# Prompt attention: the value product of a block moved one turn later in TensorE's hand-written order

## The chip, the cores and the metric

The kernel runs on one core of a Trainium2 chip. The metric is the device time of one execution in microseconds (us). Of three runs of the kernel before, the median is 4370.94 us (4367.86 to 4372.69).

## The reference, cut to what matters

The program is one inference step of a two-layer hybrid decoder trunk: in each layer three mixers (a state-space mixer, latent attention, gated linear attention) and a gated feed-forward part, for a prompt of 1024 tokens and for 8 sample tokens that attend to a cache of 8192 positions. The change touches only the latent attention of the prompt: 8 heads, 1024 queries, causal, softmax in float32.

```python
def _attn_block(q_lat, q_pe, q_pos, ckv, kpe, k_pos):
    s = (jnp.einsum('bqhl,bkl->bhqk', q_lat, ckv) + jnp.einsum('bqhr,bkr->bhqk', q_pe, kpe))
    mask = (k_pos[None, :] <= q_pos[:, None])[None, None]
    s = jnp.where(mask, s * MLA_SCALE, NEG_INF)
    p = jax.nn.softmax(s, axis=-1)
    return jnp.einsum('bhqk,bkl->bqhl', p, ckv)
...
    o = jnp.einsum('bshl,lhv->bshv', o_lat, w_uv)
```

## The kernel before, in words

`trunk` runs seven stages in each of two layers; `mla_prompt` is the fourth. Each stage is a block in which every engine has an instruction stream written out by hand, and semaphores order them. Nothing is scheduled by a planner: an engine does what its stream says, in that order, and waits where the stream says `wait_ge`.

In the main loop of the stage the work is cut into 128 units in all (64 a layer). A unit is one head and one block of 128 queries: four pairs of heads p, and in each pair 16 turns v. An even v is the first head of the pair with query block q = 7, 6, ... 0; an odd v is the second head with q = 0, 1, ... 7. A unit with block q looks at n = q + 1 blocks of 128 keys, so big and small units alternate: n = 8, 1, 7, 2, 6, 3, 5, 4, 4, 5, 3, 6, 2, 7, 1, 8. Unit u is turn v = u modulo 16 of pair p.

What is done for a unit, with the line of the instruction that the profile shows:

- scores (TensorE, L1197): queries by keys into PSUM banks 0 and 1 (even u) or 2 and 3 (odd u).
- maxima (VectorE, L1382, L1383, L1386): causal mask added to the last block, the row maximum, its negative times the scale.
- exponentials (ScalarE, L1295): exp into the SBUF tile prob, with the row sum; two tiles in turn.
- transposes (TensorE, L1209): n transposes of prob into banks 4 and 5 in turn, at most four to a bank.
- copies (VectorE, L1402): the transposed blocks to the SBUF tile pT; two tiles in turn.
- reciprocals (VectorE, L1392): one over the row sum.
- values (TensorE, L1219): n products of pT with the values, 64 columns wide, accumulated in bank 6, which is the only bank for it. `values(u)` waits for the copies of u and, since the bank must be empty, for `output(u - 1)` (semaphore e_oe).
- output (ScalarE, L1303): bank 6 times the reciprocal into the tile otok. `output(u)` waits for the reciprocal and for the product.

Two more kinds of work share the turns. In turns 2 to 12 of pairs 0 to 2 `step` computes queries and keys of the next pair in 11 steps (TensorE L1160, L1163, L1166, L1169, L1174; they all use bank 7). A letter per step says who empties the bank, D for VectorE (`drain`, L1353 to L1374) and A for ScalarE (L1279): DAAADDDAAAD. Every step waits until the step before it is drained. Step 6 (turn 8) has the longest drain: VectorE first computes two products, then two sums of 1032 columns (L1364) and eight small copies (L1370). And `outputs` (TensorE L1183, ScalarE L1285 and L1287) transposes a finished half of a pair's result in turn 14 and in turn 1 of the next pair.

The order within a turn before the change:

- TensorE: transposes of u, scores of u + 2, values of u, [outputs], [step]
- ScalarE: exponentials of u + 2, output of u, [outputs], [drain of an A step]
- VectorE: copies of u, reciprocal of u, maxima of u + 2, [drain of a D step]. `reciprocals(u)` waits for `output(u - 2)`, since the two share a slot of two.

Of the kernel before, what the change touches and what calls it, by code (L numbers as in the profile page):

```python
# [87 lines left out]
class Trunk:  # L88
# [63 lines left out]
    def T(self, i, n=1):  # L152

        return self.big[:, i * TOKENS:(i + n) * TOKENS]
# [846 lines left out]
    def mla_prompt(self):  # L1001
# [58 lines left out]
        NU = len(units)  # L1060
# [21 lines left out]
        def drained(eng, k):  # L1082
            eng.wait_ge(e_xa if kinds[k] == "A" else e_xd, kinds[:k + 1].count(kinds[k]))
# [6 lines left out]
        with nc.Block() as block:  # L1090
# [38 lines left out]
            def _(pe):  # L1129
# [48 lines left out]
                def outputs(p, half):  # L1178
                    k = out_of[p, half]
                    drained(pe, k - 1)  # L1180
                    pe.wait_ge(e_oe, NV * p + (12, 16)[half])
                    for i, q in enumerate(((2, 3, 4, 5), (0, 1, 6, 7))[half]):
                        last = pe.transpose(ps[:, 7, i * P:(i + 1) * P], otok[p % 2][:, q, :], ident)  # L1183
                    last.then_inc(e_ax, 1)

                def scores(u):
                    p, z, q = units[u]
                    if u % NV == 0:
                        drained(pe, step_of[p, 6])
                        drained(pe, step_of[p, 9])  # L1190
                        pe.wait_ge(d_kp, 4)
                    if u >= 2:
                        pe.wait_ge(e_p, u - 1)
                    n = (q + 1) * P
                    for c in range(0, n, 512):
                        w = min(512, n - c)
                        last = pe.matmul(ps[:, 2 * (u % 2) + c // 512, 0:w], query[p % 2][z][0:KQ, q * P:(q + 1) * P],  # L1197
                                         keys[p % 2][z][0:KQ, c:c + w], start=True, stop=True)
                    last.then_inc(e_s, 1)

                def transposes(u):
                    p, z, q = units[u]
                    pe.wait_ge(e_p, u + 1)
                    for g in range(banks_of[u]):
                        at = first_bank[u] + g
                        if at >= 2:
                            pe.wait_ge(e_te, at - 1)
                        for kb in range(4 * g, min(4 * g + 4, q + 1)):
                            last = pe.transpose(ps[:, 4 + at % 2, (kb % 4) * P:(kb % 4 + 1) * P], prob[u % 2][:, kb * P:(kb + 1) * P], ident)  # L1209
                        last.then_inc(e_t, 1)  # L1210

                def values(u):
                    p, z, q = units[u]
                    pe.wait_ge(e_te, first_bank[u + 1])
                    if u >= 1:
                        pe.wait_ge(e_oe, u)
                    h = 2 * p + z
                    for kb in range(q + 1):
                        last = pe.matmul(ps[:, 6, 0:V_DIM], pT[u % 2][:, kb * P:(kb + 1) * P], vt[:, kb, h * V_DIM:(h + 1) * V_DIM],  # L1219
                                         start=(kb == 0), stop=(kb == q))  # L1220
                    last.then_inc(e_o, 1)
# [16 lines left out]
                for u in range(NU):  # L1238
                    p, v = u // NV, u % NV
                    transposes(u)  # L1240
                    if u + 2 < NU:
                        scores(u + 2)
                    values(u)
                    if v == 1 and p:
                        outputs(p - 1, 1)
                    if 2 <= v < 2 + NS and p + 1 < PAIRS:
                        step(p + 1, v - 2)
                    if v == 14:
                        outputs(p, 0)
                outputs(PAIRS - 1, 1)  # L1250

            @block.scalar
            def _(act):
                for dst, src in ((15, 11), (13, 9), (14, 10)):
                    act.activation(T(dst), T(src), ACT.Square).then_inc(d_sq, 1)
                act.wait_ge(d_var, 1)
                act.activation(r2, r2, ACT.Sqrt).then_inc(d_sd, 1)
                act.wait_ge(d_var, 2)
                act.activation(rstd[:, :], rstd[:, :], ACT.Sqrt).then_inc(d_sd, 1)
                for q in range(2):  # L1260
                    act.wait_ge(d_tr, q + 1)
                    act.activation(ct[:, 4 * q:4 * q + 4, :].rearrange("p t c -> p (t c)"), ps[:, 3 + q, :], ACT.Copy).then_inc(d_tre, 1)
                act.wait_ge(d_tr, 3)
                act.activation(ct[0:8, QT, :], ps[0:8, 5, 0:P], ACT.Copy).then_inc(d_tre, 1)
                act.activation(self.ct_s, ps[0:8, 5, 0:P], ACT.Copy)
                act.wait_ge(d_tr, 4)
                act.activation(kt[:, 0:QT, :].rearrange("p t c -> p (t c)"), ps[:, 6, 0:QT * ROPE], ACT.Copy).then_inc(d_tre, 1)
                act.wait_ge(d_tr, 5)
                act.activation(kt[0:8, QT, :], ps[0:8, 7, 0:ROPE], ACT.Copy).then_inc(d_tre, 1)
                act.activation(self.ckv_s, T(11)[:, SEQ:TOKENS], ACT.Copy)  # L1270
                act.activation(self.kpe_s, T(4)[0:ROPE, SEQ:TOKENS], ACT.Copy)

                def drain(p, j):
                    k, w = step_of[p, j], p % 2
                    bank = 2 + k % 6 if p == 0 else 7
                    act.wait_ge(e_ax, k + 1)
                    for z in range(2):
                        to = query[w][z][0:NOPE, chunk(j - 1)] if j < 4 else keys[w][z][0:NOPE, kchunk(j - 7)]
                        last = act.activation(to, ps[64 * z:64 * z + 64, bank, 0:to.shape[1]], ACT.Copy)  # L1279
                    last.then_inc(e_xa, 1)  # L1280

                def outputs(p, half):
                    act.wait_ge(e_ax, out_of[p, half] + 1)
                    if half == 0:
                        act.activation(hc[:, 2 + p, 256:768], ps[:, 7, :], ACT.Copy).then_inc(e_xa, 1)  # L1285
                    else:
                        act.activation(outer(hc[:, 2 + p, 0:SEQ]), ps[:, 7, :].rearrange("p (a c) -> p a c", a=2), ACT.Copy).then_inc(e_xa, 1)  # L1287

                def exponentials(u):
                    p, z, q = units[u]  # L1290
                    act.wait_ge(e_nb, u + 1)
                    if u >= 2:
                        act.wait_ge(e_t, first_bank[u - 1])
                    n = (q + 1) * P
                    act.activation(prob[u % 2][:, 0:n], ps[:, 2 * (u % 2):2 * (u % 2) + 2, :].rearrange("p b n -> p (b n)")[:, 0:n],  # L1295
                                   ACT.Exp, bias=st[:, u % 2:u % 2 + 1], scale=MLA_SCALE,
                                   accum_out=st[:, 2 + u % 2:3 + u % 2]).then_inc(e_p, 1)

                def output(u):
                    p, z, q = units[u]  # L1300
                    act.wait_ge(e_r, u + 1)
                    act.wait_ge(e_o, u + 1)
                    act.activation(otok[p % 2][:, q, z * V_DIM:(z + 1) * V_DIM], ps[:, 6, 0:V_DIM], ACT.Copy,  # L1303
                                   scale=st[:, 4 + u % 2:5 + u % 2]).then_inc(e_oe, 1)
                for j in (1, 2, 3, 7, 8, 9):
                    drain(0, j)
                act.wait_ge(d_out, 64)
                exponentials(0)
                for t in range(0, QT, 2):
                    act.wait_ge(e_vm, t + 1)  # L1310
                    act.activation(vt[:, t, :], ps[:, 4, :], ACT.Copy).then_inc(e_va, 1)
                    if t == 0:
                        exponentials(1)
                for u in range(NU):
                    p, v = u // NV, u % NV
                    if u + 2 < NU:
                        exponentials(u + 2)
                    output(u)
                    if v == 1 and p:
                        outputs(p - 1, 1)  # L1320
                    if 2 <= v < 2 + NS and p + 1 < PAIRS and STEPS[v - 2] == "A":
                        drain(p + 1, v - 2)
                    if v == 14:
                        outputs(p, 0)
                outputs(PAIRS - 1, 1)

            @block.vector
# [896 lines left out]
```

## Time and profile before

| | us |
|---|---|
| median of three runs | 4370.94 |
| the profiled execution | 4382.27 |
| its span in the profile | 4380.6 |
| main loop of the prompt attention, layer 0 (546 to 792 us) | 246 |
| main loop of the prompt attention, layer 1 (2700 to 2944 us) | 244 |

Over the whole span TensorE's matmuls are busy 3606.5 us (82%), weight loads 3033.2 (69%), VectorE 1946.7 (44%), ScalarE 909.6 (21%), GpSimd 309.5 (7%). The shares are means over seven different stages; the change lies in one of them, so the two loops are read by themselves. A row of a timeline gives the start in us from the span's start, the duration, the engine, the line, the operation, the tiles and shapes, and in brackets how long the engine had been idle and for whom it waited. Matmul records overlap a little: the next instruction starts some 0.15 us before the one before it is shown as ended.

### The profile page before, as it was taken

The numbers are of one execution on the slowest core, as the hardware profiler recorded it, in microseconds if no ns is written. First come the engines' busy times: TensorE is split into PE (matmuls) and PEld (weight loads), VectorE is DVE, ScalarE is ACT, GpSimd is POOL, SyncE is SP. The second block draws the span as 40 slices with busy tenths as digits, with TensorE's granted clock in tenths as the row PEclk, the third lists the DMA queues.
The fourth block names the chain that finished last, engine by engine and source line by source line (L and its number), as shares of the span: only waits on it lengthen the run. The fifth ranks groups of instructions, "written<-read, shape, count | busy, mean of one in ns | idle before, by whom it ended". The sixth has DMA issues, their size and how long they took to land. (4 is left out here: it accounts for less than half of the span.)

```text
span 4380.6 us, 51760 instructions
## 1 busy us (share of the span) xinstructions
PE 3606.5 (82%) x20008; PEld 3033.2 (69%) x20008; DVE 1946.7 (44%) x3586; ACT 909.6 (21%) x1552; POOL 309.5 (7%) x366
## 2 busy tenths in 40 slices
PE   6974688566688999999999557875677889999997
PEld 4632466455577999999856234654555879999996
DVE  2453666333343544544451646652333344454443
ACT  2013233222221211111111032321222121111112
POOL 2000000222200000000010000003222000000000
PEclk9986799788898999999999658987898999999999
DMA  4111100333310111111121101004222111111111
GB/s 91 25 23 28 28 4 1 99 96 96 94 41 21 54 44 44 58 38 50 24 43 31 28 8 28 4 21 127 89 78 73 39 41 49 44 59 40 49 34 51
DMA packets 227424, 207.29 MB, mean 47 GB/s; under 512 B 51252, under 2 KB 196788, under 8 KB 227012
## 3 DMA queue, kind: packets, MB, share of 16 engines
q1 hardware_dynamic: 200584, 119.11, 10.1%
q0 software_dynamic: 26624, 85.11, 6.7%
q8 instruction: 159, 2.61, 0.3%
q14 instruction: 57, 0.47, 0.0%
HBM read 193.31 MB, written 11.05 MB: 47 GB/s over the span
## 5 line engine op out<-in xcount | busy, mean ns | idle before, releaser
L185 PE MATMUL ps<-streamH,upH 128*128 128x344 f32 x2112 | 451.4, 322 | 36.0 <-DVE streamL L2041 29.7
L185 PE MATMUL ps<-streamH,upL 128*128 128x344 f32 x2112 | 449.1, 321 | 0.0
L185 PE MATMUL ps<-streamL,upH 128*128 128x344 f32 x2112 | 447.6, 320 | 0.0
L185 PEld LDWEIGHTS ps<-streamH,upH 128*128 128x128 f32 x2112 | 356.0, 189 | 40.7 <-issue 34.7
L173 PE MATMUL ps<-hc,wring 128*128 128x344 f32 (+1 forms) x1248 | 366.5, 457 | 21.0 <-DVE hc L410 21.0
L1570 PE MATMUL ps<-kH,qpart 128*128 128x512 f32 x256 | 137.7, 538 | 287.5 <-DVE kL L1682 183.2
L185 PEld LDWEIGHTS ps<-streamH,upL 128*128 128x128 f32 x2112 | 357.7, 189 | 0.0
L185 PEld LDWEIGHTS ps<-streamL,upH 128*128 128x128 f32 x2112 | 354.3, 189 | 0.0
L173 PEld LDWEIGHTS ps<-hc,wring 128*128 128x128 f32 (+1 forms) x1248 | 230.3, 185 | 156.1 <-issue 44.2
L2088 DVE TENSOR_TENSOR xT<-xT,ps 128x1032 f32<-128x1032 f32 x176 | 216.1, 1229 | 240.2 <-PE ps L185 240.2
L1982 ACT ACTIVATE upH<-hc 128x1024 fp32r<-128x1024 f32 x88 | 93.3, 1062 | 981.1 <-PE ps L185 981.1
L1570 PEld LDWEIGHTS ps<-kH,qpart 128*128 128x128 f32 x256 | 53.5, 209 | 339.4 <-DVE kL L1682 229.2
L1682 DVE TENSOR_TENSOR kL<-ps,kH 128x512 fp32r<-128x512 f32 x256 | 173.6, 690 | 251.2 <-ACT kH L1618 211.3
L1618 ACT ACTIVATE kH<-ps 128x512 fp32r<-128x512 f32 x256 | 149.8, 597 | 533.7 <-DMA out_new_gla_prompt<-wring 187.7
L1588 PEld LDWEIGHTS ps<-big,wring 128*64 128x64 f32 x2048 | 222.7, 137 | 24.2 <-issue 22.7
L1588 PE MATMUL ps<-big,wring 128*64 128x128 f32 x2048 | 230.4, 273 | 1.1 <-DVE wring L1706 1.1
L1219 PEld LDWEIGHTS ps<-big 128*128 128x128 f32 x1152 | 148.8, 200 | 118.7 <-DVE big L1402 99.2
L2056 DVE COPY hc<-ps 128x1032 f32<-128x1032 f32 x44 | 54.3, 1233 | 376.2 <-PE ps L185 376.2
L1219 PE MATMUL ps<-big 128*128 128x64 f32 x1152 | 158.3, 285 | 70.0 <-DVE big L1402 36.3
L185 PE MATMUL ps<-hidH,downH 128*128 128x344 f32 x960 | 203.5, 320 | 0.8 <-DVE xT L2088 0.8
L185 PE MATMUL ps<-hidL,downH 128*128 128x344 f32 x960 | 202.6, 319 | 0.0
L185 PE MATMUL ps<-hidH,downL 128*128 128x344 f32 x960 | 202.5, 319 | 0.0
(423 smaller groups left out, 5603.1 us busy)
## 6 DMA issues: line engine op xcount, KB each, us to landing
hc<-in_w_ffn_in SPq DMA_DIRECT2D x88, 512.0 KB
hc<-in_w_ffn_out SPq DMA_DIRECT2D x44, 512.0 KB
wring<-in_w_in SPq DMA_DIRECT2D x22, 512.0 KB, 3.9
stream_raw<-in_w_out SPq DMA_DIRECT2D x16, 512.0 KB, 3.9
big<-in_x_prompt SPq DMA_DIRECT2D x1, 4096.0 KB
out_y_prompt<-big SPq DMA_DIRECT2D x8, 512.0 KB
scratch_y<-hc SPq DMA_DIRECT2D x16, 136.0 KB
scratch_u<-wring SPq DMA_DIRECT2D x4, 516.0 KB
```

The lines of the kernel that those rows point to most:

```text
L173: last = pe.matmul(self.ps[0:lhsT.shape[1], bank + n, 0:NCOL], lhsT, rhs[:, n * NCOL:(n + 1) * NCOL], start=(k == 0), stop=(k == len(pairs ...
L185: last = pe.matmul(self.ps[:, bank + n, 0:NCOL], w, x[:, n * NCOL:(n + 1) * NCOL], start=(k == 0 and i == 0), stop=(k == len(terms) - 1 an ...
L1219: last = pe.matmul(ps[:, 6, 0:V_DIM], pT[u % 2][:, kb * P:(kb + 1) * P], vt[:, kb, h * V_DIM:(h + 1) * V_DIM], start=(kb == 0), stop=(kb = ...
L1570: pe.matmul(ps[:, 4 + slot, :], qpart[:, b * P:(b + 1) * P], kH[b % 2][:, :], start=(b == 0), stop=False)
L1588: last = pe.matmul(ps[0:64, 7, 0:P], own(pTp[:, j, :], b), KB[k][b][:, key * P:(key + 1) * P], start=(b == 0 and j == 0), stop=(b == SAMPL ...
L1618: act.activation(kH[b % 2][:, :], ps[:, b % KBANKS, :], ACT.Copy).then_inc(f_kh, 1)
L1682: TT(kL[b % 2][:, :], ps[:, b % KBANKS, :], kH[b % 2][:, :], ALU.subtract).then_inc(f_kte, 1)
L1982: act.activation(upH[u][:, :, :], raw[u], ACT.Copy).then_inc(g_wh[u], 1)
L2056: dve.tensor_copy(n3(g[t][:, 2:]), self.psn(3)).then_inc(g_gc, 1)
L2088: TT(n3(xT[:, n, :]), n3(xT[:, n, :]), self.psn(3 * ((n + 1) % 2)), ALU.add).then_inc(g_ev, 1)
```

## The change

Two of the three streams of the main loop get another order, nothing else changes: no instruction is added or removed, no tile, bank or semaphore is other than before. TensorE computes `values(u - 1)` where it computed `values(u)`, and ScalarE copies `output(u - 1)` out where it copied `output(u)`. Both have the last unit left over after the loop. VectorE's stream is as before.

```diff
                     transposes(u)
                     if u + 2 < NU:
                         scores(u + 2)
-                    values(u)
+                    if u >= 1:
+                        values(u - 1)
                     if v == 1 and p:
                         outputs(p - 1, 1)
                     if 2 <= v < 2 + NS and p + 1 < PAIRS:
                         step(p + 1, v - 2)
                     if v == 14:
                         outputs(p, 0)
+                values(NU - 1)
                 outputs(PAIRS - 1, 1)
...
                     if u + 2 < NU:
                         exponentials(u + 2)
-                    output(u)
+                    if u >= 1:
+                        output(u - 1)
...
                     if v == 14:
                         outputs(p, 0)
+                output(NU - 1)
                 outputs(PAIRS - 1, 1)
```

The order within a turn is then: TensorE transposes of u, scores of u + 2, values of u - 1, [outputs], [step]; ScalarE exponentials of u + 2, output of u - 1, [outputs], [drain]; VectorE copies of u, reciprocal of u, maxima of u + 2, [drain].

## Rows read from the trace of the kernel before

**Rows 1.** Windows: length, busy PE, PEld, DVE, ACT, POOL; PEclk, DMA share, GB/s
```profile
546.00:792.00 246.00, 209.24 (x1187) 156.37 (x1187) 151.46 (x407) 85.26 (x232) 0.00 (x0) 0.94 0.01 2
2700.00:2944.00 244.00, 208.41 (x1183) 155.90 (x1183) 151.28 (x407) 84.48 (x231) 0.00 (x0) 0.94 0.01 2
```

**Rows 2.** Waits of TensorE's matmuls, 548 to 788 us: total, times, longest
```profile
PE ps L1219 <- DVE big L1402: 18.1, 10, 4.1
PE ps L1219 <- ACT wring L1303: 16.6, 18, 1.8
```

**Rows 3.** Timeline of turns 4 and 5 of pair 3, layer 0, no steps
```profile
752.84 0.82 PE L1209 MATMUL ps<-cst,big 128*128 128x128 f32 x6
...
753.50 1.25 PE L1197 MATMUL ps<-big 96*128 96x512 f32 x4
...
754.58 1.53 PE L1219 MATMUL ps<-big 128*128 128x64 f32 x12
754.78 0.30 DVE L1382 TENSOR_TENSOR ps<-ps,cst 128x128 f32<-128x128 f32 x1 [0.21 <-PE ps L1197]
...
756.17 0.80 ACT L1295 ACTIVATE big<-ps,wring 128x640 f32<-128x640 f32 x1 [2.28 <-DVE wring L1386]
...
756.95 0.30 ACT L1303 ACTIVATE wring<-ps,wring 128x64 f32<-128x64 f32 x1
...
757.40 0.85 PE L1219 MATMUL ps<-big 128*128 128x64 f32 x6
...
758.09 0.72 PE L1209 MATMUL ps<-cst,big 128*128 128x128 f32 x5
```

**Rows 4.** Groups by line and form, 548 to 788 us, longest and shortest forms
```profile
L1402 DVE COPY big<-ps 128x512 f32<-128x512 f32 x47 | 31.9, 690 | 34.3 <-PE ps L1209 32.6 <-DVE wring L1358 1.6
...
L1383 DVE TENSOR_REDUCE wring<-ps 128x1 f32<-128x1024 f32 x7 | 8.6, 1225 | 0.2
...
L1295 ACT ACTIVATE big<-ps,wring 128x1024 f32<-128x1024 f32 x7 | 7.8, 1114 | 24.2 <-DVE wring L1386 24.2
...
L1295 ACT ACTIVATE big<-ps,wring 128x128 f32<-128x128 f32 x7 | 2.6, 368 | 0.4
...
L1383 DVE TENSOR_REDUCE wring<-ps 128x1 f32<-128x128 f32 x7 | 2.0, 292 | 0.2
```

**Rows 5.** Timeline: one step of the next pair and the transposes after it
```profile
620.81 1.38 PE L1163 MATMUL ps<-big,wring 128*128 128x344 f32 x4
...
622.02 0.82 PE L1209 MATMUL ps<-cst,big 128*128 128x128 f32 x6
```

**Rows 6.** Timeline: first transposes of pairs 0 to 3, step 6's drain, values ahead of pair 3
```profile
546.35 1.07 PE L1209 MATMUL ps<-cst,big 128*128 128x128 f32 x8 [0.83 <-issue]
...
608.86 1.04 PE L1209 MATMUL ps<-cst,big 128*128 128x128 f32 x8
...
643.71 2.46 DVE L1364 TENSOR_TENSOR big<-wring 32x1032 f32<-32x1032 f32 x2
...
648.58 2.39 PE L1219 MATMUL ps<-big 128*128 128x64 f32 x10 [4.14 <-DVE big L1402]
...
673.15 1.04 PE L1209 MATMUL ps<-cst,big 128*128 128x128 f32 x8
...
737.40 1.97 PE L1219 MATMUL ps<-big 128*128 128x64 f32 x16 [1.40 <-ACT wring L1303]
...
739.21 1.50 PE L1209 MATMUL ps<-cst,big 128*128 128x128 f32 x8
```

**Rows 7.** Timeline of pair 3: turn 14's transposes, and the loop's last instruction
```profile
783.29 0.28 PE L1209 MATMUL ps<-cst,big 128*128 128x128 f32 x1
...
791.39 0.60 ACT L1287 ACTIVATE hc<-ps 128x512 f32<-128x512 f32 x1 [1.00 <-PE ps L1183]
```

**Rows 8.** Busy time by window, after step 6 and where pair 3 begins
```profile
650.00:654.00 4.00, 4.00 (x15) 2.90 (x14) 0.97 (x4) 2.16 (x5) 0.00 (x0) 0.50 0.00 0
...
738.00:742.00 4.00, 4.00 (x23) 3.18 (x23) 1.45 (x3) 0.61 (x3) 0.00 (x0) 0.70 0.03 6
```

## The prediction

> **What bounds the kernel now.** I read the windows first, then the waits, then the timeline. The two loops that the change touches last 246 and 244 us, 11% of the span, and TensorE's matmuls are busy 209 and 208 us of them [rows 1]. So about 36 us a loop is all that any order could win if nothing else moved: 72 us, or 1.6% of the time. The waits say what that idle time is [rows 2]: in layer 0, values wait 18.1 us for the copies of their own unit (10 times, 4.1 us at most) and 16.6 us (18 times) for ScalarE's output, that is, for bank 6 to be emptied. The change aims at the first. TensorE is also not at full speed: its granted clock is 0.94 over both loops [rows 1], and as it has two levels (1.2 and 2.4 GHz), 2 x 0.06 x 246 = 30 us of a loop run at half clock. One such stretch follows the long drain of step 6, one lies where pair 3 begins [rows 8].
>
> **A turn in numbers.** In the timeline [rows 3] transposes of n = 6 blocks take 753.50 - 752.84 = 0.66 us, so T(n) = 0.11 n. Scores of n = 5 take 1.08, so S(n) = 0.215 n. Values of n = 6 take about 1.32, so V(n) = 0.22 n. What TensorE ends is seen by another engine 0.2 us later (754.58 to 754.78). Maxima: mask 0.30, the reduction, negative 0.15 and small gaps, so with 0.29 us at n = 1 and 1.23 at n = 8 [rows 4] M(n) = 0.67 + 0.134 n; for n = 5 that is 1.34, and the row shows 756.17 - 754.78 = 1.39 with the hop. Exponentials: 0.37 to 1.11 us, E(n) = 0.26 + 0.107 n [rows 4]. Output 0.30, and 0.15 from its end to the values that wait for it (757.25 to 757.40, rows 3). A copy of 4 blocks 0.69 [rows 4]. A step of kind L1163 takes 622.02 - 620.81 = 1.21 us [rows 5].
>
> With these I carried the streams along: every instruction starts at the latest of its engine's previous end and its waits. Applied to the old order in turns 4 and 5 of pair 3 this gives 5.22 us; the row shows 758.09 - 752.84 = 5.25 [rows 3]. So the arithmetic is good to about 0.05 us per two turns, as long as the clock is full.
>
> **Part 1: values one turn later.** In the old order the ring that returns to itself every two turns is, for a big unit u + 2: S(u+2), maxima, exponentials, output(u), then values(u+1), then T(u+2). ScalarE does output behind the exponentials, so whatever values come next wait for those exponentials. Next were values(u + 1), a small unit, while the big values(u) lay before the wait, under the maxima of u + 2. That is good cover: V(8) = 1.76 us hides maxima of 1.61. In the new order values(u - 1), small, lie under the maxima, and the big values(u) wait for output(u - 1), which stands behind the same exponentials. **The wait for bank 6 is not removed, it is put in front of the big product instead of the small one.** Worked for turns 2 and 3 of pair 3 (n = 7, 2; clock full, T(2) starting at 7.45 us of a pair starting at 0): S(4) ends 9.51, maxima 9.71 to 11.18, exponentials to 12.12, output(1) to 12.42, values(2) 12.56 to 14.10, and only then T(4). TensorE has nothing from 10.60 to 12.56. The two turns take 6.65 us; the same hand in the old order gives 5.55. In the middle of a pair (n = 4, 5), where neighbours are equal, new and old agree within 0.1; at its end the new order is again 0 to 0.7 behind.
>
> The starts of the transposes of a pair without steps come out at 0, 4.15, 7.45, 9.73, 14.10, 16.28, 19.98, 22.05, 25.14, 27.63, 30.35, 33.62, 36.45, 40.41, 43.34, 48.4 and 50.05 (next pair).
>
> **Part 2: where steps lie in the turns.** In pairs 0 to 2 a step of 1.21 us stands between values(u - 1) and the next transposes. If it lies in the idle time it costs nothing, and here it often does. The worst place of the old order is step 6: VectorE sums for 2.46 us (643.71) and copies 1.4 more before it reaches the copies of turn 9, and values(9) start at 648.58 after 4.14 us of nothing [rows 6]. In the new order TensorE goes on with values(8), waits about 1.1 us for the drain, does step 7, waits 1.5 us for a transpose bank, does T(10) and S(12), then waits 2.3 us for output(8) behind late exponentials. The stall is split and about 1 us shorter, no more, because VectorE's order is the same and maxima(11) are as late as before. A stepped pair comes out at 0, 4.15, 7.89, 10.28, 15.75, 19.14, 22.86, 26.14, 29.97, 33.15, 37.6, 43.90, 47.38, 51.20, 54.13, 59.20, 60.84.
>
> **The sum at full clock.** The pairs take 62.51 (608.86 - 546.35), 64.29, 66.06 and, to the end of the loop (791.39 + 0.60), 52.78 us [rows 6, 7]: 245.6. With the half-clock stretches taken out by the same hand the old order is 61.4, 62.3, 62.3 and 49.45 = 235.4 (turns 9 to 16 of pair 1, 30.7 us in the trace, come out at 28.7), so half clock costs 10.2 us a loop, 0.35 us per us of it. The new order gives 58.4 for pair 0 (no older values are owed in its turn 0), twice 60.84, and 54.2 for pair 3, in whose end values(15) and both outputs stand behind values(13) and (14); in the old order the stretch from turn 14 on takes 8.7 us [rows 7], in the new 10.9. Sum 234.3, **1.1 us less per loop, 2 us in all: nothing.** The pairs with steps win 3.0, 1.4 and 1.4, the one without loses 4.8.
>
> **Part 3: the clock.** What the idle time looks like does change. TensorE's holes become longer where the work around them is thin: 1.0 us in turn 1 between two V(8), 1.9 in turn 3, 1.6 in turn 12, 1.3 in turn 14, against 16.6 / 18 = 0.9 on average in the old order [rows 2] and 1.40 at its place ahead of a pair [rows 6]. The trace of before shows that such places can cost clock: after the hole of 1.4 us ahead of pair 3 the clock fell (0.70 in 738 to 742, rows 8), with transposes of 8 blocks at 1.50 us for 1.04 [rows 6], while at the same place ahead of pairs 1 and 2 the transposes kept their 1.04 us. No row prices the new holes; the bounds are none of them bringing it down (0), and two more falls in each of eight pairs. A short fall is about 3.4 us at half clock (0.70 of 742 and the next window), times 0.35 = 1.2 us; so 0 to 19 us. I take 1.5 falls a pair, 12 falls, 14 us, since the rows after the nearest hole show falls and the new holes are deeper.
>
> The Trainium skill, "TensorE: Matmul & The Clock Gate", section "A second HAM failure mode: psum-queue depth-cycling", says that a TensorE which idles briefly but often between groups of matmuls goes back and forth between the clocks. The trace agrees (0.94 in both loops, with 0.50 and 0.70 in the windows shown). By it the upper half of this part's bounds would be the likely one, 10 to 19 us. The skill's "Perfetto Trace Analysis", section "Optimizing Tensor Performance", wants independent groups of matmuls to rotate through banks so that emptying one overlaps the next; values have one bank, and the 18 waits for it are what the row shows. By it this change would leave that wait whole.
>
> **Part 4: the rest.** No instruction is added. ScalarE's drains of A steps stand behind output(u - 1) where they stood behind output(u); both are ready by then. VectorE's reciprocal of u now waits for output(u - 2), one turn later than before, and the maxima of u + 2 are queued behind it: 0.1 to 1.2 us in turns with small n, all inside the starts above. The other stages are untouched: 0.
>
> **The sum.** Profiled execution: 4382.3 - 2 + 14 = 4394; it lay 11.3 above the median, so on the median's scale 4370.9 - 2 + 14 = 4383.
>
> **The rivals.**
> - A, forecast: schedule even, clock falls more often. 4375 to 4392, likeliest 4383. Chance 0.50.
> - B: the holes bring no further falls (in 2 of 3 places the 1.4 us hole did not). Then -2, with 4 us of error in the hand sums: 4362 to 4374. Chance 0.23.
> - C, the other side: the copies' wait goes and nothing takes its place. It needs ScalarE's output to be ready when the big values come. All of it is 18.1 x 2 = 36 us: 4335; if the stretches at half clock after step 6 also shorten without the rest, half is 4350. Against it: the ring of turns 2 and 3. For it: the 4.14 us stall is the largest single one, and pair 0 wins 3 us. It decides where output(u - 1) ends before S(u + 3) does. Chance 0.12.
> - D: two or more falls a pair, so that the big products behind the holes run at half clock (V(8) at 3.5 us), and the reciprocal's wait hits oftener than I have it: 19 us of clock and 5 a loop: 4371 + 29 = 4400. Chance 0.15.
>
> That it does nothing (the order is as it was) can't be: the streams are in order. The measurement can tell 0.2%, about 9 us. Faster by more: C, 0.12. Within: B and the low part of A, 0.23 + 0.07 = 0.30. Slower: 0.43 + 0.15 = 0.58. The range takes in A, B and D's centre: 4360 to 4401.
>
> **What would show it.** Waits of L1219 for the copies near 0; its waits for L1303 up from 16.6 to some 35 us or more a loop; new waits of L1209 (for exponentials or copies) and of step 7; two turns at v = 2 of pair 3 at 6.6 us for 5.6; pair 3 4 to 5 us longer, pairs 0 to 2 shorter except where the clock falls; granted clock of the loops at 0.90 to 0.92. The forecast is wrong if values still start without a hole in turn 3, or if the clock stays at 0.94 or rises.

## The result, and the profile after

The changed kernel takes 4393.53 us in the median of five runs (4390.60 to 4395.58) against 4372.69 (4367.86 to 4373.53): ratio 1.0048, 95% interval 1.0036 to 1.0061. It is slower by 21 us, 0.48%. The forecast was slower, 4383, and 12 us. Medians here and below leave out one slow run, the 5002.81 us of a fill_before execution.

The profiled execution has a span of 4392.5 us (4380.6 before). The two loops of the prompt attention, from the first transposes of pair 0 to the end of the last copy of outputs, take 255.2 us each for 245.6: 2 x 9.6 = 19.2 us, nearly the whole. The rest of the program differs from profile to profile: from the end of the first loop to the start of the second it takes 1902 us in the shortest and 1916 in the longest, though no kernel changes it. So below I read the loops. They repeat well: those of layer 0 and layer 1 agree within 0.1 us in every kernel but act_only (511.2 and 504.5).

The windows of the changed kernel (start and end, length, busy time of PE, PEld, DVE, ACT, POOL, granted clock, DMA), to be read beside [rows 1]:

```profile
546.00:800.00 254.00, 213.67 (x1183) 162.02 (x1183) 151.99 (x407) 85.19 (x230) 0.00 (x0) 0.91 0.01 2
...
2706.00:2958.00 252.00, 212.02 (x1174) 160.71 (x1172) 150.14 (x405) 85.51 (x231) 0.00 (x0) 0.91 0.01 2
```

The same work takes 4 us more busy time and there is more idle time, and the clock is 0.91 for 0.94. How much of a loop runs at half clock is read below from the pairs, where two decimals tell more.

The waits in layer 0 (total, times, longest), to be read beside [rows 2]:

```profile
PE ps L1219 <- ACT wring L1305: 30.9, 22, 2.9
...
DVE wring L1396 <- ACT wring L1305: 19.2, 21, 1.3
...
PE ps L1209 <- DVE big L1406: 4.2, 3, 1.4
...
PE ps L1169 <- DVE big L1368: 3.0, 3, 1.1
...
PE ps L1219 <- DVE big L1406: 0.6, 1, 0.6
```

The wait that the change aimed at is gone: 18.1 us of values for copies are 0.6. In its place values wait 30.9 us for ScalarE's output, 16.6 before; VectorE's reciprocals wait for the same output, 19.2 us, 0 before; and transposes and step 7 wait 7.2 us for the slow drain of step 6.

The timeline of turns 2 and 3 of pair 3 of the changed kernel shows the new wait at its place:

```profile
749.29 0.93 PE L1209 MATMUL ps<-cst,big 128*128 128x128 f32 x7
...
751.75 0.81 PE L1197 MATMUL ps<-big 96*128 96x384 f32 x2
...
753.06 0.90 ACT L1297 ACTIVATE big<-ps,wring 128x768 f32<-128x768 f32 x1 [2.97 <-DVE wring L1390]
...
753.95 0.31 ACT L1305 ACTIVATE wring<-ps,wring 128x64 f32<-128x64 f32 x1
...
754.40 1.75 PE L1219 MATMUL ps<-big 128*128 128x64 f32 x14 [1.85 <-ACT wring L1305]
...
755.99 0.83 PE L1209 MATMUL ps<-cst,big 128*128 128x128 f32 x6
```

Output(1) stands in ScalarE's stream behind the exponentials of unit 4, and the big values(2), 14 records for n = 7, wait for it with nothing else to do for 1.85 us. From the transposes of turn 2 to those of turn 4 it is 755.99 - 749.29 = 6.70 us.

The stations of layer 0, to be read beside [rows 6, 7]:

```profile
546.88 1.07 PE L1209 MATMUL ps<-cst,big 128*128 128x128 f32 x8 [0.83 <-issue]
...
611.35 1.07 PE L1209 MATMUL ps<-cst,big 128*128 128x128 f32 x8
...
676.45 1.07 PE L1209 MATMUL ps<-cst,big 128*128 128x128 f32 x8
...
741.34 1.07 PE L1209 MATMUL ps<-cst,big 128*128 128x128 f32 x8
...
801.50 0.60 ACT L1289 ACTIVATE hc<-ps 128x512 f32<-128x512 f32 x1 [0.81 <-PE ps L1183]
```

The pairs take 64.5, 65.1, 64.9 and 60.8 us for 62.5, 64.3, 66.1 and 52.8. Pairs 0 to 2 together lose 1.6 us, pair 3, which has no steps, loses 8.0.

The windows of the four pairs of layer 0 (columns as above), first of the kernel before:

```profile
546.35:608.86 62.51, 53.34 (x303) 39.29 (x304) 40.33 (x108) 21.95 (x60) 0.00 (x0) 0.97 0.04 6
608.86:673.15 64.29, 54.78 (x310) 40.73 (x309) 40.32 (x108) 22.90 (x62) 0.00 (x0) 0.95 0.00 1
673.15:739.21 66.06, 56.90 (x310) 42.18 (x309) 40.32 (x108) 22.98 (x62) 0.00 (x0) 0.92 0.00 1
739.21:791.99 52.78, 44.20 (x272) 34.14 (x271) 30.25 (x82) 17.42 (x48) 0.00 (x0) 0.92 0.00 1
```

and of the changed kernel:

```profile
546.88:611.35 64.47, 55.10 (x288) 40.75 (x288) 39.20 (x104) 21.48 (x57) 0.00 (x0) 0.89 0.03 6
611.35:676.45 65.10, 55.43 (x309) 41.47 (x309) 40.28 (x109) 23.14 (x63) 0.00 (x0) 0.92 0.00 1
676.45:741.34 64.89, 55.48 (x310) 41.46 (x309) 40.37 (x109) 23.17 (x63) 0.00 (x0) 0.92 0.00 1
741.34:802.10 60.76, 48.52 (x288) 38.86 (x287) 31.44 (x87) 18.32 (x52) 0.00 (x0) 0.89 0.00 1
```

Twice what the clock lacks of 1, times the length, is the time at half clock: 3.8 + 6.4 + 10.6 + 8.4 = 29.2 us of the loop before and 14.2 + 10.4 + 10.4 + 13.4 = 48.4 of the changed one, 19.2 more, and 38 more in the two loops.

### The profile page after: what moved, and what is told of

Its sections match the earlier page's. It is cut to its first block and busy times, and to the rows that moved or that the text cites. A ratio compares the mean times of both kernels' runs of the same rounds, so it can differ in the third digit from the quotient of the medians.

```text
span 4392.5 us, 51760 instructions
## 1 busy us (share of the span) xinstructions
PE 3625.9 (83%) x20008; PEld 3054.5 (70%) x20008; DVE 1947.1 (44%) x3586; ACT 910.6 (21%) x1552; POOL 308.0 (7%) x366
## 5 line engine op out<-in xcount | busy, mean ns | idle before, releaser
L1219 PEld LDWEIGHTS ps<-big 128*128 128x128 f32 x1152 | 154.1, 205 | 104.6 <-DVE big L1406 54.8
L2060 DVE COPY hc<-ps 128x1032 f32<-128x1032 f32 x44 | 54.2, 1233 | 376.9 <-PE ps L185 376.9
L1219 PE MATMUL ps<-big 128*128 128x64 f32 x1152 | 159.1, 287 | 63.3 <-ACT wring L1305 62.4
```

Source lines behind the costliest of these rows:

```text
L2060: dve.tensor_copy(n3(g[t][:, 2:]), self.psn(3)).then_inc(g_gc, 1)
```

## The experiments

All times are medians, each beside the kernel before on the same chip. "Loop" is the time from the first transposes to the last copy of outputs in layer 0 of the profile. Where the lines of a kernel have moved, its rows have line numbers of their own.

The letters stand for these causes of the loss. G: output(u - 1) stands behind the exponentials of u + 2 and keeps bank 6 from the big values. R: VectorE's reciprocal waits for that output and delays the maxima. K: late values cost clock whatever ScalarE does. F: the clock is no cause, and only the schedule counts. H: holes go on costing clock in any order, so that filling them always wins.

### The change in some pairs only: new_012 and new_3

```diff
-                    if u >= 1:
+                    if u >= 1 and u - 1 < 3 * NV:       # new_3: u - 1 >= 3 * NV
                         values(u - 1)
+                    if not u < 3 * NV:                   # new_3: not u >= 3 * NV
+                        values(u)
```

and the same for output in ScalarE's stream.

> The change in pairs 0 to 2 only (those with steps), the old order in pair 3. In the trace of the changed kernel these three pairs take 64.5, 65.1 and 64.9 us for 62.5, 64.3 and 66.1 before, +1.6 a loop: 4374 us (4368 to 4380). The prediction's sum had them winning 5.8 us a loop at full clock and losing it to the clock: 4365 to 4375. If the loss were spread evenly over the pairs (three quarters of 21 us): 4387.

> The change in pair 3 only (no steps), the old order in pairs 0 to 2. In the trace of the changed kernel pair 3 takes 60.8 us for 52.8, +8 a loop: 4387 us (4381 to 4391). The prediction's sum gives +4.8 at full clock and some clock: 4381 to 4386. If the loss were even over the pairs: 4376.

new_012: ratio 1.0021 (1.0013 to 1.0030), +10.5 us; loop 249.7, its pairs 64.5, 65.1, 64.9 and 55.3. new_3: ratio 1.0052 (1.0039 to 1.0065), +23.2 us; loop 255.8, its pairs 62.5, 64.3, 66.1 and 63.0. Both lie above the ranges, which against the kernel before were -3 to +9 and +10 to +20 us. Pairs 0 to 2 take in new_012 what they took in the changed kernel, and pair 3 of new_3 takes 2.2 us more than there. So the loss is local: some 2 us a loop in the three pairs with steps, 8 to 10 in the pair without. Neither is a gain, and the two do not add up to the whole (33.7 for 20.8): where one order hands over to the other, pair 3 takes 2.2 us (new_3) and 2.5 us (new_012) more, 4.7 a loop. In new_3 that goes with the clock, 0.80 over pair 3 for 0.89. Half of new_012's loss is the handover.

### ScalarE's half alone: act_only

```diff
                         exponentials(u + 2)
-                    output(u)
+                    if u >= 1:
+                        output(u - 1)
```

with TensorE's order as before.

> ScalarE's half alone: values of u in their turn as before, the output one turn later behind the exponentials of the next but one unit. Now values(u + 1) wait for output(u), which stands behind exponentials of u + 3, whose scores were only just issued: nothing covers maxima, exponentials and output. By hand 0.67 + 0.134 n + 0.26 + 0.107 n + 0.45 = 2.5 us a unit at n = 4.5, less 0.5 for what is waited for today: 2.0 x 128 = 256 us more, 4570 to 4680 against 4371. Rival (the output's place matters little, since both kernels wait for it): within 40 us of before.

Ratio 1.1195 (1.1172 to 1.1218), +522 us, 213 more than the end of the range (+309). The loop takes 511 us. The direction and the mechanism are as expected, the size is not. Its waits over the loop, and three rows of its timeline:

```profile
PE ps L1219 <- ACT wring L1303: 165.6, 61, 6.2
```

```profile
565.84 0.58 ACT L1295 ACTIVATE big<-ps,wring 128x384 f32<-128x384 f32 x1 [6.23 <-DVE wring L1388]
...
566.41 0.31 ACT L1303 ACTIVATE wring<-ps,wring 128x64 f32<-128x64 f32 x1
566.87 1.09 PE L1219 MATMUL ps<-big 128*128 128x64 f32 x4 [2.17 <-ACT wring L1303]
```

The window over its whole loop (columns as above; the granted clock is the 0.63):

```profile
548.00:1058.00 510.00, 342.72 (x1186) 247.56 (x1183) 153.81 (x406) 85.27 (x231) 0.00 (x0) 0.63 0.01 1
```

Values wait 2.17 us for an output behind fresh exponentials. Over the loop their waits, for copies and output, grow from 34.7 to 166.8 us: 132 us, for 2.0 x 64 = 128 by hand. The other half of the 266 us that the loop lost is the clock: it is 0.63, that is, 2 x 0.37 x 511 = 378 us at half clock, and there a product takes twice its time (4 records of values 1.09 us, for 0.56 at full clock in the changed kernel). I had counted all of it at full clock.

### TensorE's half alone, and where the drains stand: pe_only, out_first, old_pe_out_first

pe_only is the new TensorE stream with ScalarE's old stream. out_first has ScalarE's operations in this order:

```diff
+                    if u >= 1:
+                        output(u - 1)
                     if u + 2 < NU:
                         exponentials(u + 2)
-                    if u >= 1:
-                        output(u - 1)
```

> TensorE's half of the change alone: values one turn later, ScalarE's stream as before (exponentials of u + 2, then output of u), so that output(u - 1) stands ahead of exponentials(u + 2). Theory G (the loss comes from the big values waiting for an output that stands behind fresh exponentials): by hand V(2) of pair 3 starts right behind S(5), T(4) at 12.3 us instead of 14.10, the pair some 9 us shorter than in the changed kernel, the loops 8 us each below before: 4350 to 4362 us against 4371 before. TensorE's waits of L1219 for the output under 10 us a loop (31 in the changed kernel). Rival K (values one turn later leave TensorE with thin work around its holes whatever ScalarE does, and the clock pays): 4388 to 4398, as the changed kernel.

> The changed kernel with ScalarE's two operations of a turn swapped: output of u - 1, then exponentials of u + 2; drains stay behind both. Theory G: as the run before, and a little better, as the drains of A steps do not stand behind output(u): 4348 to 4360 us. Rival K: 4388 to 4398. A third case, the exponentials are now late behind an output that waits for big values (V(8) 1.76 us against maxima of 0.80 where the next unit is small): 4370 to 4385.

> TensorE's order as in the kernel before (values of u in their own turn), ScalarE's order as in out_first: output of u - 1, exponentials of u + 2, then drains. It tells whether the 35 us a loop that out_first gained over before are TensorE's part or ScalarE's. Theory S (ScalarE's place of the output carries most of it): values no longer wait for an output behind exponentials, only for the copies (18 us a loop in before); loop 225 to 232 us against 245.6, that is 27 to 40 us off the time. Theory T (values one turn later carry most of it): loop 238 to 245.

pe_only: ratio 0.9998 (0.9989 to 1.0006), -1.4 us, loop 244.4, pairs 62.4, 68.9, 68.4 and 44.7. out_first: 0.9854 (0.9838 to 0.9870), -65.3 us, loop 210.9, pairs 53.5, 57.5, 55.2 and 44.7. old_pe_out_first: 1.0051 (1.0037 to 1.0065), +22.9 us, loop 255.4, pairs 69.2, 65.9, 71.1 and 49.3. None lies in its range: pe_only was put at 9 to 21 us of gain, out_first at 11 to 23, old_pe_out_first at 27 to 40 or, by theory T, at a loop of 238 to 245.

Pair 3 gives the verdict on theory G. The wait of values for the output over pe_only's loop, and pair 3 of pe_only and of old_pe_out_first, both at full clock (1.00):

```profile
PE ps L1219 <- ACT wring L1305: 0.4, 1, 0.4
...
745.83:790.52 44.69, 41.98 (x286) 34.06 (x286) 30.83 (x87) 19.01 (x52) 0.00 (x0) 1.00 0.01 1
```

```profile
753.41:802.67 49.26, 40.70 (x272) 31.78 (x271) 30.11 (x82) 17.35 (x48) 0.00 (x0) 1.00 0.00 1
```

With TensorE's half alone pair 3 takes 44.7 us, 8.1 less than before, and 16.1 less than with both halves, and the wait for the output is 0.4 us a loop for 16.6 and 30.9. Part of this is clock. In pair 3 old_pe_out_first runs the order of before but for the two outputs, which stand one place earlier (no drain stands there to be moved), and at full clock it takes 49.3 us: so 4.6 of the 8.1 us are the order and 3.5 the half clock that is gone. So **values one turn later were good, and moving the output behind the next exponentials made them bad.** Rival K, by which the late values cost the clock whatever ScalarE does, is out.

In the pairs with steps pe_only lost what it won. I had not seen that a sequence "exponentials of u + 2, output of u" and a sequence "output of u - 1, exponentials of u + 2" are one and the same stream, and that pe_only and out_first differ only in where the drains of A steps and the copies of outputs stand. The timeline of pe_only:

```profile
625.22 0.31 ACT L1305 ACTIVATE wring<-ps,wring 128x64 f32<-128x64 f32 x1 [2.46 <-PE ps L1219]
625.43 0.90 ACT L1281 ACTIVATE big<-ps 64x344 f32<-64x344 f32 x2
...
626.39 1.42 PE L1163 MATMUL ps<-big,wring 128*128 128x344 f32 x4 [1.27 <-ACT big L1281]
```

The drain of step 1 stands behind output(3), which waits for values(3) of the next turn, and step 2 waits for the drain. With the drain ahead of that output (out_first) most of that wait is gone: TensorE waits for ScalarE's drains 3.4 + 2.0 us a loop, 22.8 in pe_only. The same move alone, in the old TensorE order, is old_pe_out_first, and my expectation of it missed: the loop is 10 us longer, not shorter. There output(u) is what the next values wait for, and it now stands behind a drain that waits for a step: values wait 21.6 us a loop for the output, 16.6 before, and 18.1 for the copies as before. The loss is all in the pairs with steps. This move pays only together with the late values. The windows of out_first:

```profile
547.00:757.00 210.00, 194.48 (x1187) 150.96 (x1185) 149.40 (x406) 87.00 (x231) 0.00 (x0) 0.98 0.01 3
```

TensorE is busy 93% of the loop and the clock is 0.98.

### The bank and the slot: two_after, four_slots

```diff
-                    if u >= 1:
+                    if apart(u):                      # turns 3 to 12 of pair 3
+                        pe.wait_ge(e_oe, u - 1)       # odd units use bank 7, idle there
+                        drained(pe, out_of[PAIRS - 2, 1])
+                    elif u >= 1:
                         pe.wait_ge(e_oe, u)
```

```diff
-                    if u >= 2:
-                        dve.wait_ge(e_oe, u - 1)
-                    dve.reciprocal(st[:, 4 + u % 2:5 + u % 2], ...
+                    if u >= 4:
+                        dve.wait_ge(e_oe, u - 3)
+                    dve.reciprocal(st[:, 8 + u % 4:9 + u % 4], ...
```

> The changed kernel with a second bank for values in turns 3 to 12 of pair 3 (bank 7, idle there), so that values(u) wait for output(u - 2) in place of output(u - 1). Theory G (the wait of the big values for the output behind fresh exponentials is what pair 3 lost): pair 3 falls from 60.8 to 48 to 53 us, the time 15 to 25 us below the changed kernel's, about that of before. Rival R (the reciprocal's wait for the output, and with it the maxima, is the bound): pair 3 stays above 58 us.

> The changed kernel with four slots for the reciprocal in place of two, so that reciprocals(u) wait for output(u - 4) and VectorE's maxima no longer stand behind output(u - 2). It takes away VectorE's 19.2 us a loop of waits for the output and leaves the wait of values for bank 6. Theory G (values behind the output behind the exponentials carry the loss): the loop falls by 0 to 5 us from 255.2, the time stays 12 to 21 us above before. Rival R (the reciprocal's wait carries it): by more than 8 us a loop, the time within 4 us of before or below.

two_after: ratio 1.0010 (1.0001 to 1.0020), +5.0 us, 16 less than the change; loop 249.3, pair 3 at 54.8 for 60.8. Theory G asked for 48 to 53 and R for more than 58; it lies between, nearer to G. In turns 3 to 12 the holes before values are gone, and the transposes of turn 12 start 34.21 us after those of turn 0, for 36.93 in the changed kernel: 2.7 us, at full clock in both:

```profile
742.26:776.47 34.21, 30.90 (x209) 24.83 (x208) 24.10 (x70) 12.74 (x38) 0.00 (x0) 1.00 0.01 1
```

Two things are left: T(u + 2) then wait for the exponentials themselves, and turn 14, where bank 6 is alone again and the hole comes at once:

```profile
781.78 0.28 PE L1211 MATMUL ps<-cst,big 128*128 128x128 f32 x1
...
784.48 0.30 ACT L1310 ACTIVATE wring<-ps,wring 128x64 f32<-128x64 f32 x1
...
784.93 2.75 PE L1224 MATMUL ps<-big 128*128 128x64 f32 x14 [2.87 <-ACT wring L1310]
```

four_slots: ratio 1.0061 (1.0047 to 1.0074), +26.1 us, above theory G's range of 12 to 21; loop 260.4, that is 5 us longer than the changed kernel and not 0 to 5 shorter. Pairs 0 to 2 are unchanged (64.4, 65.0, 64.9) though VectorE's waits there, 12.8 of the 19.2 us, are gone, so in them the reciprocal's wait is not what sets the time. Pair 3 became longer, 66.0:

```profile
739.29:805.33 66.04, 55.47 (x286) 44.28 (x286) 31.04 (x87) 18.37 (x51) 0.00 (x0) 0.75 0.00 1
```

Half of it, 33 us, is at half clock, for 13.4 in the changed kernel. Up to the transposes of turn 9 it is level with the changed kernel (27.94 us after its first for 28.11). Then comes the same hole of 1.28 us ahead of the values done in turn 10 in both, and here the clock falls behind it (10 records of values take 2.14 us for 1.30). So the loss is not the reciprocal's: R is out as the cause. Why the clock fell here and not there is open, and in the rest of pair 3 the clock hides what the wait itself was worth.

### The clock by itself: fill_before, fill_after

```diff
+                def fill(n, bank):
+                    for _ in range(n):
+                        pe.matmul(ps[:, bank, 0:256], ident, self.cst[:, 0:256], start=True, stop=True)
...
                         scores(u + 2)
+                    if v == 9 and p < 3:
+                        fill(8, 1)
+                    elif v in (12, 15):
+                        fill(2, 2 * (u % 2) + 1)
                     values(u)
```

> The kernel before with such idle products in turn 9 of pairs 0 to 2 (8 of them, 3.4 us, in the hole of 4.14 us) and 2 each in turns 12 and 15. Theory H: the loops fall from 245.6 to the hand sum at full clock, 235.4 (234 to 239), 14 to 22 us off the time. Rival F: loops stay at 245 to 248.

> The changed kernel with idle products put into TensorE's holes ahead of its waits (1 to 4 products of 128x256 with the identity, some 0.43 us each, into a half of a scores bank that nobody reads): turns 1, 3, 9, 10, 12 and turn 5 of pair 3. They are work that the reference does not ask for and leave the result alone. Each lot is shorter than the hole that it lies in. Theory H (half clock costs the changed loops 255.2 - 234.3 = 21 us each, 234.3 being the hand sum at full clock): the loops fall to 234 to 242 us, the granted clock to 0.97 or more, the time to 13 to 20 us below the kernel before's. Rival F (the clock falls are beside the point, the waits alone set the time): loops stay at 255 or grow.

fill_before: ratio 0.9949 (0.9932 to 0.9966), -21.2 us; loop 235.2 for 245.6. fill_after: 0.9969 (0.9956 to 0.9982), -13.3 us; loop 239.3 for 255.2. fill_after has 1 to 4 such products ahead of the waits in turns 1, 3, 9, 10 and 12, and in turn 5 of pair 3. Both came out in their ranges. The pairs of fill_before take 61.2, 61.9, 61.6 and 50.5 us, those of fill_after 59.8, 61.5, 61.1 and 56.9. More work on the busiest engine made both faster. Their windows, fill_before first, fill_after second:

```profile
546.00:780.00 234.00, 214.76 (x1265) 162.26 (x1263) 150.85 (x406) 83.92 (x231) 0.00 (x0) 0.99 0.01 2
```

```profile
548.00:786.00 238.00, 223.58 (x1304) 172.26 (x1302) 151.22 (x406) 85.37 (x232) 0.00 (x0) 0.98 0.01 2
...
778.00:786.00 8.00, 6.77 (x40) 6.12 (x39) 1.45 (x3) 1.61 (x5) 0.00 (x0) 0.72 0.00 1
```

No instruction that the result needs was moved; the idle time was filled and the clock stayed up (0.99 and 0.98 for 0.94 and 0.91). Rival F is out.

The two runs also give the price of half clock. fill_before has 2 x 0.01 x 234 = 4.7 us of it left, 24.5 less than before, and its loop is 10.4 us shorter: 0.42 us per us. fill_after has 2 x 0.02 x 238 = 9.5 left, 38.9 less, and its loop is 15.9 us shorter: 0.41. The price is the same in both orders. With what is left taken off at 0.41, the loops at full clock are 235.2 - 1.9 = 233.3 us in the old order and 239.3 - 3.9 = 235.4 in the new: the new one is about 2 us longer. This is an estimate: the idle products may delay work themselves (the transposes of turn 12 of pair 3 start 0.2 us later in fill_after than in the changed kernel), and the clock has two decimals. Part of the difference is seen without it. The first twelve turns of pair 3 ran at full clock in the changed kernel and in fill_before, which has the old order:

```profile
741.34:778.27 36.93, 31.37 (x209) 24.45 (x208) 24.35 (x70) 12.71 (x38) 0.00 (x0) 1.00 0.00 1
```

```profile
730.17:764.42 34.25, 30.98 (x204) 23.94 (x204) 24.01 (x65) 12.20 (x35) 0.00 (x0) 1.00 0.01 1
```

The new order is 2.7 us longer there, by its waits alone.

### Versions that beat both: out_first_fill, late_copies

out_first with idle products around step 6, and out_first with the eight small copies of step 6's drain behind turn 10:

```diff
                     if 2 <= v < 2 + NS and p + 1 < PAIRS and STEPS[v - 2] == "D":
                         drain(p + 1, v - 2)
+                    if v == 10 and p + 1 < PAIRS:
+                        rope_copies(p + 1)
```

> out_first with idle products (128x256 by the identity, as in fill_after) in the two holes that are left around step 6: 2 before step 7, 3 before the transposes of turn 10, pairs 0 to 2. Theory H: the stretch at half clock behind step 6 (3 a loop) goes, 2 to 4 us a pair: loop 200 to 205 us against 210.9. Rival F: loop stays at 210 to 212.

> out_first with the eight small copies of step 6's drain (1.42 us of VectorE ahead of the copies of turn 9) moved behind turn 10. The hole of 1.40 us before the transposes of turn 10 goes, 1.0 to 1.4 us a pair at full clock, and if with it the half clock behind step 6, 3 us more: loop 198 to 208 us against 210.9. If VectorE's later work is then what TensorE waits for, nothing is won: 210 to 212.

out_first_fill: ratio 0.9903 (0.9887 to 0.9918), -41.4 us; loop 210.6, so filling wins nothing once the order leaves few holes (theory H is wrong here). H had counted on half clock in three pairs, but out_first has it in pair 1 alone. Its time is 24 us worse than out_first's with equal loops; it is lost in other stages and what causes that is open. late_copies: ratio 0.9822 (0.9808 to 0.9835), -79.4 us, 4291.66 against 4371.09; loop 206.3, 39.3 less than before. It is the fastest run. The transposes of turn 10 no longer wait:

```profile
632.82 0.89 DVE L1410 COPY big<-ps 128x512 f32<-128x512 f32 x2
...
632.85 0.84 PE L1169 MATMUL ps<-big,wring 128*128 128x344 f32 x2 [1.19 <-DVE big L1368]
633.66 0.52 PE L1209 MATMUL ps<-cst,big 128*128 128x128 f32 x3
...
636.71 1.42 DVE L1383 COPY wring<-big 32x8 f32<-32x8 f32 x8
```

## Why the prediction was right, and where its size was off

- What bounds the loop, and the hand arithmetic: right. T(2) to T(4) of pair 3 was put at 6.65 us and takes 6.70. The transposes of turns 4, 6, 8, 10 and 12 of that pair lie at 14.65, 20.57, 25.70, 30.79 and 36.93 us after its first, for 14.10, 19.98, 25.14, 30.35 and 36.45 by hand: the constant 0.5 us is the outputs of turn 1, which the list for a pair without steps leaves out. The list for a pair with steps holds within 0.2 us up to turn 9 (pair 1: 33.20 for 33.15) and is 1.8 us early at turn 10, behind the drain of step 6 (39.43 for 37.6).
- "The wait for bank 6 is put in front of the big product": right, and the sharpest statement. The wait grew from 16.6 to 30.9 us; I had said 35 or more. act_only and pe_only isolate it, and pe_only and out_first bring it to 0.4 us with the same one bank.
- Copies' wait near zero, new waits of L1209 and of step 7, clock of the loops 0.90 to 0.92: right (0.6, 4.2 and 3.0 us a loop, 0.91). Rival C (the copies' wait goes and nothing replaces it) is refuted; so is B (no more half clock).
- Pairs 0 to 2 shorter, pair 3 longer by 4 to 5: half right. Pair 3 lost 8.0; pairs 0 to 2 lost 1.6 together where the sum gave them a win of 5.8 at full clock. The clock took most of that, not all.
- The clock, Part 3, put at 14 us in all: it came to about 16. The amount was right: 12 falls of 3.4 us are 41 us, the windows of the pairs show 38. The price was 0.35 us per us and is 0.41 by the fill runs. The amount is in part luck: 1.5 falls a pair was a choice between 0 and 2 that no row fixed, and the falls do not lie where the holes were listed. In layer 0 the clock fell behind the hole of turn 12 in all four pairs and behind that of turn 14 in pair 3, but behind that of turn 3 in pair 0 alone. There the transposes after 1.74 us of nothing take 1.49 us; in pair 3, after 1.85 us, the same 6 blocks take 0.83 (755.99, above). Rows of pair 0, turn 4, and of pair 1, turns 2, 10 and 12 to 14:

```profile
561.22 1.49 PE L1209 MATMUL ps<-cst,big 128*128 128x128 f32 x6
...
619.30 0.93 PE L1209 MATMUL ps<-cst,big 128*128 128x128 f32 x7
...
650.78 0.52 PE L1209 MATMUL ps<-cst,big 128*128 128x128 f32 x3 [1.40 <-DVE big L1406]
...
663.17 1.52 PE L1219 MATMUL ps<-big 128*128 128x64 f32 x12 [1.46 <-ACT wring L1305]
...
665.18 1.75 PE L1209 MATMUL ps<-cst,big 128*128 128x128 f32 x7
...
666.73 2.76 PE L1197 MATMUL ps<-big 96*128 96x512 f32 x4
```

After the hole of 1.46 us the transposes of 7 blocks take 1.75 us for 0.93 (619.30) and the largest scores 2.76 us. The rule of the Trainium skill that the prediction weighed ("TensorE: Matmul & The Clock Gate", "A second HAM failure mode: psum-queue depth-cycling") put this term into the upper half of its bounds, 10 to 19 us; the trace agrees, at about 16.

- **The term that was mis-sized most is the schedule at full clock:** -1.1 us a loop by hand, -2 in all. The loops lost 19.2 us, of which the clock is about 38 x 0.41 = 16, so 3 to 4 are the schedule; the fill runs give the same, +2 a loop. The errors are small and lie all over. In pairs 1 and 2 the fill runs have the new order ahead by 0.4 us each where the hand had 1.4: the old order was put too long (62.3 us for 61.9 and 61.6), the new one too short (60.84 for 61.5 and 61.1). Pair 3 at full clock takes 49.3 us in the old order, 49.45 by hand, but about 60.8 - 0.41 x 13.4 = 55.3 in the new, 54.2 by hand. The hand arithmetic had been held against two turns of one pair at full clock; over 16 turns its error is up to about 1 us a pair.
- Both errors, and some 2 us outside the loops, go the same way, so 12 us became 21. The result lies 1.5 us above the band of rival A, between it and D. A's cause holds (11 more falls in eight pairs, not 16). D's second half, that the reciprocal waits oftener than Part 4 has it (0.1 to 1.2 us in turns with small n), came true: 19.2 us in 21 turns, 1.3 at most; but four_slots shows that in pairs 0 to 2 it costs nothing.
- The profiled execution was put at 4394 and took 4394.13. That is luck: its two loops lost 19.2 us for the forecast's 12, and the rest of it happened to be 7 us shorter than in the profile before.

## What to carry to other kernels

When a product is moved in one engine's stream, ask which instruction it now waits for and what stands before that one in its own engine's stream: here the move was worth 8 us in a pair, and the partner's move behind a longer instruction turned it into a loss of 8, the clock included in both. Two streams are the same if only their loop bounds are cut elsewhere; what differs is where the occasional work (drains, outputs) stands, and that was worth 33.5 us a loop (244.4 to 210.9). Price a hole of TensorE with the clock that it may cost behind it: here a us at half clock cost 0.41 us in either order. Whether the clock falls could not be told from the length of the hole: 1.85 us in turn 3 of pair 3 passed, 1.46 us in turn 12 of pair 1 did not. A hand sum needs a term for its own error: held against two turns it was good to 0.05 us, over a pair to about 1.

## What the runs showed of the hardware that I had not expected

Idle matmuls in the holes made the kernel faster, by 21 us of 4374 in the old order, though TensorE is its busiest engine. Behind holes of 1.5 to 2.9 us the clock fell to half in some turns and not in others, and the cost of half clock was the same in both orders, 0.42 and 0.41 us per us by the fill runs. One hole of 1.28 us, at the same place of pair 3, was passed at full clock in the changed kernel and brought the clock down in four_slots. With a hole in nearly every turn (act_only) the granted clock of the whole loop was 0.63 and the loop took twice its time.
